# Solving the delta rule's triangular blocks of 16 instead of 8 by substitution, in a two-block transformer kernel

## The reference

```python
decay = jnp.exp(jnp.where(causal, g_cum[..., :, None] - g_cum[..., None, :], -jnp.inf))
k_beta = k * beta[..., None]
lower = jnp.where(strict, jnp.einsum('bhncd,bhnmd->bhncm', k_beta, k) * decay, 0.0)
t_inv = lax.linalg.triangular_solve(lower, eye, left_side=True, lower=True, unit_diagonal=True)
u = jnp.einsum('bhncm,bhnme->bhnce', t_inv, v * beta[..., None])
w = jnp.einsum('bhncm,bhnmd->bhncd', t_inv, k_beta * jnp.exp(g_cum)[..., None])
```

## Time and profile before

| | |
|---|---|
| median of three runs | 1306.01 us |
| the profiled execution's own time | 1305.88 us |
| its span, first to last instruction | 1304.5 us |
| PE busy | 1296.4 us, 99% |
| DVE busy | 931.3 us, 71% |
| ACT busy | 716.4 us, 55% |
| POOL busy | 89.8 us, 7% |
| TensorE's granted clock, mean | 0.999 of 2.4 GHz |
| the stage of the change, laps 0 to 7 | about 622 to 864 us |

### The profile page before, as it was taken

One profiled execution on the slowest core, in us unless ns is written; L12 is line 12 of the kernel. 1 busy time (PEld: TensorE's weight loads), 2 busy tenths in 40 slices (PEclk: granted clock), 3 DMA queues, 4 the chain that ended last, 5 costly groups with the idle time before them and its releaser, 6 DMA issues.

```text
span 1304.5 us, 23151 instructions
## 1 busy us (share of the span) xinstructions
PE 1296.4 (99%) x9404; PEld 1172.2 (90%) x9404; DVE 931.3 (71%) x1598; ACT 716.4 (55%) x1257; POOL 89.8 (7%) x181
## 2 busy tenths in 40 slices
PE   9999999999999999999999999999999999999998
PEld 8988999998879999989999999888999888989896
DVE  7866887777877977777877788864666555765553
ACT  7655665556666655547666666653343443644442
POOL 1000000000000000000122233300000000000000
PEclk9999999999999999999999999999999999999999
DMA  8443465543434655544444443556544444465540
GB/s 332 162 162 130 162 226 194 178 183 135 152 111 156 221 193 193 186 170 146 134 139 133 136 125 106 158 180 223 195 170 170 161 170 177 177 228 193 184 139 33
DMA packets 35036, 219.25 MB, mean 168 GB/s; under 512 B 4209, under 2 KB 7665, under 8 KB 9457
## 3 DMA queue, kind: packets, MB, share of 16 engines
q1 hardware_dynamic: 30608, 211.83, 44.7%
q10 hardware_dynamic: 4320, 5.94, 3.0%
HBM read 215.78 MB, written 1.05 MB: 166 GB/s over the span
## 4 chain that ended last, share of the span: by engine, by line
PE 96%; DVE 1%; ACT 1%; issue 0%; DMA 0%; SPq 0%; POOL 0%; ACTq 0%; DVEq 0%; POOLq 0%
PE bank L326 29%; PE bank L328 28%; PE bank L327 28%; PE bank L718 1%; PE bank L769 1%; PE bank L444 1%; PE bank L1756 1%; PE bank L1773 1%; PE bank L790 1%; DMA sb_x<-x 0%; PE bank L2445 0%; PE bank L712 0%; PE bank L1636 0%; PE bank L1912 0%; PE bank L1626 0%
## 5 line engine op out<-in xcount | busy, mean ns | idle before, releaser
L326 PE MATMUL bank<-sb_h_hi,sb_w_hi 128*128 128x256 f32 x1504 | 430.3, 286 | 0.0
L327 PE MATMUL bank<-sb_h_lo,sb_w_hi 128*128 128x256 f32 x1504 | 419.7, 279 | 0.0
L328 PE MATMUL bank<-sb_h_hi,sb_w_lo 128*128 128x256 f32 x1504 | 419.6, 279 | 0.0
L286 DVE TENSOR_TENSOR sb_w_lo<-sb_raw,sb_w_hi 128x1024 fp32r<-128x1024 f32 x185 | 226.2, 1223 | 105.7 <-ACT sb_w_hi L278 105.4
L326 PEld LDWEIGHTS bank<-sb_h_hi,sb_w_hi 128*128 128x128 f32 x1504 | 282.4, 188 | 5.5 <-issue 3.6
L327 PEld LDWEIGHTS bank<-sb_h_lo,sb_w_hi 128*128 128x128 f32 x1504 | 282.0, 188 | 2.8 <-issue 1.4
L328 PEld LDWEIGHTS bank<-sb_h_hi,sb_w_lo 128*128 128x128 f32 x1504 | 282.4, 188 | 0.0
L278 ACT CAST sb_w_hi<-sb_raw 128x1024 fp32r<-128x1024 f32 x188 | 197.0, 1048 | 100.0 <-PE bank L328 98.2
L289 DVE TENSOR_TENSOR sb_w_lo<-sb_raw,sb_w_hi 128x1024 fp32r<-128x1024 f32 x185 | 225.7, 1220 | 0.0
L279 ACT CAST sb_w_hi<-sb_raw 128x1024 fp32r<-128x1024 f32 x188 | 197.6, 1051 | 0.0
L326 PE MATMUL bank<-sb_w_hi,sb_h_hi 128*128 128x256 f32 (+1 forms) x512 | 161.2, 315 | 0.0
(11 more groups left out here) (378 smaller groups left out, 1922.2 us busy)
## 6 DMA issues: line engine op xcount, KB each, us to landing
sb_raw<-stream SPq DMA_DIRECT2D x199, 1024.0 KB, 4.8
sb_row<-rows ACTq DMA_DIRECT2D x3, 512.0 KB, 3.8
sb_x<-x SPq DMA_DIRECT2D x4, 256.0 KB, 4.5
sb_raw<-stream SPq DMA_DIRECT2D x2, 512.0 KB, 5.9
sb_norm_b<-norm_b ACTq DMA_DIRECT2D x4, 256.0 KB, 4.3
out<-sb_x SPq DMA_DIRECT2D x4, 256.0 KB, 2.0
sb_g_row<-sb_g_rows ACTq DMA_DIRECT2D x7, 128.0 KB, 6.3
sb_retain<-retain ACTq DMA_DIRECT2D x1, 768.0 KB, 4.2
```

The costliest lines, as they stand in the source:

```text
L286: V.tensor_tensor(w_lo[:, b, 0:HALF], raw[:, r, 0:HALF], w_hi[:, b, 0:HALF].bitcast(F32), ALU.subtract).then_inc(lo_done, 1)
L326: T.matmul(out_ap, l_hi, r_hi, start=start, stop=False, **kw)
L327: T.matmul(out_ap, l_hi, r_lo, start=False, stop=False, **kw)
L328: return T.matmul(out_ap, l_lo, r_hi, start=False, stop=stop, **kw)
```

## The change

Substitution goes on to blocks of 16: 30 steps in place of 14, rows of up to 15 elements in place of 7. One level of doubling goes (to 16 from 8), so two are left. The spread rows are 256 elements for each of the two chunks and no longer fit `z`. They are written to the second half of `row`, where the head's output `o` also stands, so DVE now waits for `o_turned` of the head two before. PE's spread product has 512 columns in place of 128. Masks are one fewer. The orders of all four engines are written anew around this: as a rule the first level comes four half steps later on PE.

```diff
-BASE = 8
-LEVELS = 5
-MASKS = 6
+BASE = 16
+LEVELS = 4
+MASKS = 5
...
-        spread = z[:].rearrange("p (t i j) -> p t i j", t=NT, i=BASE)
+        spread = row[:, 512:1024].rearrange("p (t i j) -> p t i j", t=NT, i=BASE)
...
+            need(V, o_turned, hd - 1)
             for t in range(NT):
                 ins = V.tensor_tensor(spread[:, t], diag[:, t:t + 1, :].to_broadcast([P, BASE, BASE]),
-                                      row8.unsqueeze(2).to_broadcast([P, BASE, BASE]), ALU.mult)
+                                      row16.unsqueeze(2).to_broadcast([P, BASE, BASE]), ALU.mult)
...
-            T.matmul(bank[7][:, 0:P], same8[:], z[:], start=True, stop=True).then_inc(spread_mm, 1)
+            T.matmul(bank[7][:, :], same16[:], row[:, 512:1024], start=True, stop=True).then_inc(spread_mm, 1)
...
-            rows = bank[7][:, 0:P].rearrange("p (t i j) -> p t i j", t=NT, i=BASE)
+            rows = bank[7][:, :].rearrange("p (t i j) -> p t i j", t=NT, i=BASE)
```

PE's order in laps 1 to 3 (`delta_pe`):

```diff
                 head_unit_pe(u, 0, 0, 1, tokens)
+                head_unit_pe(u, 0, 1, 3, tokens)
+                head_unit_pe(u, 0, 3, 5, tokens)
                 level_a_pe(hd, 1)
                 flip_v_pe(hd)
-                head_unit_pe(u, 0, 1, 3, tokens)
+                head_unit_pe(u, 0, 5, 7, tokens)
                 level_b_pe(hd, 1)
-                head_unit_pe(u, 0, 3, 5, tokens)
-                level_a_pe(hd, 2)
-                head_unit_pe(u, 0, 5, 7, tokens)
-                level_b_pe(hd, 2)
...
-                level_a_pe(hd, 3)
+                level_a_pe(hd, 2)
...
-                level_b_pe(hd, 3)
+                level_b_pe(hd, 2)
```

PE's in laps 4 to 6 (`delta_pe`):

```diff
             head_unit_pe(u, 1, 0, 4)
+            head_unit_pe(u, 1, 4, 6)
+            head_unit_pe(u, 1, 6, 8)
             level_a_pe(hd, 1)
             flip_v_pe(hd)
-            head_unit_pe(u, 1, 4, 6)
-            level_b_pe(hd, 1)
-            head_unit_pe(u, 1, 6, 8)
-            level_a_pe(hd, 2)
             u = unit_d(hd, 3)
             need(T, zs_done, hd)
             head_unit_pe(u, 2, 0, 1, tokens)
+            level_b_pe(hd, 1)
+            head_unit_pe(u, 2, 1, 3, tokens)
+            level_a_pe(hd, 2)
+            head_unit_pe(u, 2, 3, 5, tokens)
             level_b_pe(hd, 2)
-            head_unit_pe(u, 2, 1, 3, tokens)
-            level_a_pe(hd, 3)
-            head_unit_pe(u, 2, 3, 5, tokens)
-            level_b_pe(hd, 3)
```

DVE's in laps 4 to 6 (`delta_dve`):

```diff
             substitute_dve(hd)
             lo()
-            level_b_dve(hd, 1)
             older_dve(n, 0, 1)
             older_dve(n, 0, 2)
             older_dve(n, 0, 3)
-            level_b_dve(hd, 2)
+            level_b_dve(hd, 1)
             outputs_dve(hd - 1)
             query_sides_dve(hd)
             vbeta_dve(hd)
-            level_b_dve(hd, 3)
+            level_b_dve(hd, 2)
```

PE's in lap 7 (`gate_a_pe`):

```diff
+            T.wait_ge(zs_done, LAST)
+            square(u + 2, 0, KD, acts, (2, 1), 0)
+            square(u + 2, 0, KD, acts, (2, 1), 1)
             level_a_pe(hd, 1)
             flip_v_pe(hd)
-            T.wait_ge(zs_done, LAST)
-            square(u + 2, 0, KD, acts, (2, 1), 0)
-            level_b_pe(hd, 1)
-            square(u + 2, 0, KD, acts, (2, 1), 1)
-            level_a_pe(hd, 2)
             T.wait_ge(sig_a, 1)
             square(u + 2, 0, KD, acts, (2, 1), 2)
-            level_b_pe(hd, 2)
+            level_b_pe(hd, 1)
```

ACT's in lap 7 (`gate_a_act`):

```diff
             hi()
+            sig_act(0, (0, 1))
             level_a_act(hd, 1)
-            sig_act(0, (0, 1))
+            hi()
             level_a_act(hd, 2)
```

More of the change, by code:

```diff
@@ L73, in constants @@
     own[:, 0:BASE] = row % BASE == np.arange(BASE)[None, :]
-    own[:, BASE:2 * BASE] = row // BASE % (HB // BASE) == np.arange(HB // BASE)[None, :]
+    own[:, BASE:BASE + HB // BASE] = row // BASE % (HB // BASE) == np.arange(HB // BASE)[None, :]
     lev.append(own)
@@ L1386, in delta_begin_dve @@
             V.tensor_scalar(cap[:], upper[:], 1.0, -NEG, ALU.subtract, ALU.mult)
-            V.tensor_copy(same8[:], levels[:, MASKS - 2, :])
-            V.tensor_copy(own8[:], levels[:, MASKS - 1, 0:2 * BASE])
-            V.tensor_copy(x8[:], levels[:, MASKS - 1:MASKS, 0:BASE].to_broadcast([P, NT, BASE]))
+            V.tensor_copy(same16[:], levels[:, MASKS - 2, :])
+            V.tensor_copy(own16[:], levels[:, MASKS - 1, 0:2 * BASE])
+            V.tensor_copy(x16[:], levels[:, MASKS - 1:MASKS, 0:BASE].to_broadcast([P, NT, BASE]))
             V.memset(xtf[HALF_ROWS[1], :, 0:HB], 0.0).then_inc(begin_done, 1)
@@ L1720, in substitute_dve @@
                     if j:
[L1721 to L1725, removed]
+                        V.wait_ge(x16_step, steps * hd + NT * (j - 1) + t + 1)
+                    so_far = x16[:, t, j + 1:BASE] if j else row16[:, 1:BASE]
+                    V.scalar_tensor_tensor(x16[:, t, j + 1:BASE], rows[:, t, j + 1:BASE, j], x16[:, t, j:j + 1], so_far,
+                                           ALU.mult, ALU.add).then_inc(x16_step, 1)
+            V.wait_ge(x16_step, steps * (hd + 1))
             for t in range(NT):
-                ins = V.tensor_tensor(xt[:, t, :].rearrange("p (b i) -> p b i", i=BASE), x8[:, t:t + 1, :].to_broadcast([P, HB // BASE, BASE]),
-                                      block8.unsqueeze(2).to_broadcast([P, HB // BASE, BASE]), ALU.mult)
+                ins = V.tensor_tensor(xt[:, t, :].rearrange("p (b i) -> p b i", i=BASE), x16[:, t:t + 1, :].to_broadcast([P, HB // BASE, BASE]),
+                                      block16.unsqueeze(2).to_broadcast([P, HB // BASE, BASE]), ALU.mult)
             ins.then_inc(inv, 1)
@@ L1989, in first_lap_levels_pe @@
             head_unit_pe(u, 2, 0, 1, tokens)
+            level_a_pe(0, 1)
+            flip_v_pe(0)
+            head_unit_pe(u, 2, 1, 2, tokens)
+            level_b_pe(0, 1)
+            head_unit_pe(u, 2, 2, 4, tokens)
             level_a_pe(0, 2)
-            head_unit_pe(u, 2, 1, 2, tokens)
+            head_unit_pe(u, 2, 4, 5, tokens)
             level_b_pe(0, 2)
[L1993 to L1996, removed]
             head_unit_pe(u, 2, 5, 7, tokens)
@@ L2127, in delta_act @@
                 hi()
-                level_a_act(hd, 4)
+                level_a_act(hd, 3)
             else:
                 hi()
-                level_a_act(hd, 1)
                 outputs_act(hd - 1)
                 load_row_act(n)
+                hi_half(0)
+                level_a_act(hd, 1)
+                silu_act(n, 0)
                 level_a_act(hd, 2)
-                hi_half(0)
-                silu_act(n, 0)
+                newest_act(n, 1)
                 level_a_act(hd, 3)
-                newest_act(n, 1)
-                level_a_act(hd, 4)
                 store_act(hd - 1)
@@ L2220, in delta_pool @@
             blocks_pool(hd, 2)
-            if RAW_V + hd >= A_HEADS and hd < A_HEADS - 1:
-                blocks_pool(hd, 3)
-                outputs_pool(hd - 1)
-                return
             if hd:
                 outputs_pool(hd - 1)
-            blocks_pool(hd, 3)
         LAST = A_HEADS - 1
@@ L2295, in gate_a_act @@
             hi()
+            sig_act(0, (0, 1))
             level_a_act(hd, 1)
-            sig_act(0, (0, 1))
+            hi()
             level_a_act(hd, 2)
-            hi()
+            store_act(hd - 1)
             level_a_act(hd, 3)
-            store_act(hd - 1)
-            level_a_act(hd, 4)
             hi()
@@ L2320, in gate_a_dve @@
             lo_half(0)
+            lo_half(1)
             level_b_dve(hd, 1)
-            lo_half(1)
             vbeta_dve(hd)
+            store_dve(hd - 1)
             level_b_dve(hd, 2)
-            store_dve(hd - 1)
-            level_b_dve(hd, 3)
             lo()
```

22 lines of the change are left out of this document (8 added, 14 removed).

## The result

The changed kernel takes **1311.42 us** (median of 6 runs, 1309.71 to 1312.56) beside 1306.17 us (6 runs, 1305.94 to 1306.33) for the kernel before on the same chip: 5.25 us more, a ratio of 1.004 [1.003, 1.005]. The forecast was 1309.3, slower, in a range of 1304.0 to 1313.0. So the sign is right and the size is 2 us short.

What follows compares the result with a forecast made beforehand. PE was taken to bound the kernel (busy 99%, 96% of the chain). Terms +0.1 + 1.9 - 0.8 + 0.8 + 1.65 = +3.6 us, less 0.3 for overlap, +3.3 on the median 1306.01: 1309.3 us, range 1304.0 to 1313.0.

Steps and rivals of the forecast that it cites:

- PE's own work: All eight heads: one doubling level less gains 1.12 us, the wider spread product costs 0.61; net gain 0.51 a head.
- DVE's steps: DVE's substitution in each head: 0.134 us a step, so sixteen more steps add 2.15 us.
- Laps 1 to 3: Heads' stretches counted from 0: PE waits of 1.15 us against a gain of 0.51, each 0.64 slower, 1.9 in three.
- The second wait: In heads' stretches 1 to 3, PE waits 0.26 us for the second half of the next weights' low part.
- Laps 4 to 6: Heads' stretches 4 to 6: a 0.24 us wait at the second level product, each gains 0.27, 0.8 in three.
- ACT's late `nwt`: DVE ends later and ACT waits for it: 0.25 us charged at the start of stretches 5, 6 and 7, 0.8 together.
- Lap 0: First head's stretch: gains of 0.51 and 0.52 (`kdec` wait) against a new low-part wait of 1.09, sum +0.06 us.
- Lap 7: Last head's stretch, beside gate A: PE idles 2.15 us for ACT's table load and sigmoid; less 0.51, 1.65 slower.
- The drain of about 1.38 us: At the sigmoid's table switch: the skill's drain would make the wait 3.5 us, the kernel 1310.7; the forecast left it out.
- the 0.3 that was taken off for waits that overlap: Deduction of 0.3 us from the +3.6 sum, for waits at the start of a head's stretch and at its levels.
- PE's work alone: Rival: DVE and ACT always in time, kernel gains 4.1 + 0.5 us, 1301.4; chance 12%, with all below 1303.4.
- DVE as the bound: Rival: none of DVE's extra work hides in seven heads' stretches, +12 us, 1318; halfway 1313.5; chance 13%.

Runs made afterwards that it cites:

- the run with the steps in the old order: The kernel before with sixteen extra substitution steps of 7 elements a head on DVE, result unread; order, spread product and three levels stay: 1319.19 us, ratio 1.0100.
- the trace with fillers: Trace of the changed kernel with 18 extra unread PE products of 256 columns ahead of the sigmoid's wait in the last head's stretch: 1311.23 us, ratio 1.0036.

## Why the prediction was right in sign and short in size

- **PE's own work** (gain 1.12, loss 0.61 a head). The spread product's chain row is the 0.86 foreseen in laps 4 to 6, where PE goes on to weight products; in laps 1 to 3, where DVE waits for its end, it is 1.14 (forecast 1.02). The forecast's 4.9 us for it is PE's own time and not what the product costs the kernel: the run with the narrow product gives back 1.7 us, since in six of eight laps PE waits for DVE instead.
- **DVE's steps.** Thirty take 4.10 us on the chain, as forecast, 0.137 each against 0.134 for the narrower ones of before. The chain of lap 2:

```profile
693.58 1.14 PE bank L1712 x2
694.75 4.10 DVE sb_d_x L1724 x30
702.06 1.23 DVE sb_w_lo L306
```

- **Laps 1 to 3** (+0.64 each): +0.66, +0.66, +0.68. Aligned by PE's starts, lap 2 loses 0.98 us from ahead of the spread to behind it (forecast 0.41 + 0.61) and 0.60 at the low part (forecast 0.48). The second wait, forecast at 0.26, is 0.1 to 0.2. The low part on the chain above is the first half, forecast at 697.83 + 2.72 = 700.55; less the 1.47 us by which the lap itself starts later, it is at 700.59. One mechanism was missed: the spreading pair takes 1.07 us, not 1.00, as it runs beside POOL.
- **Laps 4 to 6** (-0.27 each, and 0.25 for ACT's late `nwt` from lap 5 on): -0.28, -0.12, -0.15. The second L1757 waits about 0.1, not 0.24. `nwt` is on PE's load queue three times, 0.2 us of it by PE's starts in lap 5:

```profile
PEld bank L1862 <- ACT sb_d_nwt L1857: 1.0, 3, 0.5
```

- **Lap 0** (+0.06): +0.22. `kdec`'s wait went and the low part's came, 1.17 instead of 1.09.
- **Lap 7** (+1.65). The failed step. The wait is 2.09 us (forecast 2.15), between a table load at 854.90 and the sigmoid at 856.19, 1.29 behind it. The drain of about 1.38 us that the Trainium skill, "ScalarE: Activation LUTs", section "What ACT_TABLE_LOAD costs", adds to a switch doesn't stand between them here either. I priced the wait at its own length. But a standstill of this length can bring the clock down to 1.2 GHz behind it: another 1.7 us in the profiled execution, 1.6 between the two sorts of executions. Since six of ten have it, the median should have about 1 us of it.
- **The remaining 0.5 us.** From 919 to 960 us, in the attention block's products of 256 columns, the traces of the changed kernel and of all variants but one take 0.5 us more than that of before with no wait anywhere, at full clock: from 931.70 to 942.81 in the one, from 937.70 to 949.25 in the other, 11.11 and 11.55 us for the same products. The run with 14 steps has the short time, like before, and the run with the steps in the old order has the long one, so it isn't the change's order that brings it. I know no cause, and whether it belongs to a kernel or to an execution is open.

The waits, +3.7 us (0.22 + 2.00 - 0.55 + 2.07 from the trace with fillers), came within half a microsecond of the forecast's +3.3. They are nearer to the +3.6 of its sum: no run shows the 0.3 that was taken off for waits that overlap. The low clock's 1 us and the 0.5 us above would make the rest; of these the first is shown and the second is open, so that the sum fits to 0.1 us is partly luck. Of the rivals, PE's work alone is refuted by the waits in the traces and by the run with the steps in the old kernel. DVE as the bound, at 1318, is what that run shows for the old order (1319.2), not for the change's.

## What to carry to other kernels

When an edit moves work past a point where PE waits for another engine, look first at what that engine needs from PE. Here four small products issued behind two blocks of work instead of ahead of them cost 3 us, more than half of the loss, and one moved line gave it back. Price a PE standstill of some 2 us with what its clock may do afterwards, and profile more than one execution before giving that price. And a cheaper product buys little where PE next waits for DVE. Ask of each saved microsecond at which wait it would be handed back.

## What was unexpected of the hardware

The clock behind a standstill. In the delta stage of this case's traces it fell to 0.50 behind waits of 1.71, 2.09, 2.09 and 2.77 us, each time for 3.41 or 3.42 us, beginning 0.35 to 1.6 us after PE had started again. It held behind two other waits of 2.09 us, and behind all of 1.36 us and less. Two windows of the run with the steps in the old kernel, PE idle and then at half clock with PE fully busy:

```profile
639.00:641.70 2.70, 0.00 (x0) 0.00 (x0) 2.63 (x17) 0.00 (x0) 0.00 (x0) 1.00 0.55 228
642.50:644.00 1.50, 1.50 (x9) 1.50 (x8) 1.50 (x2) 0.85 (x3) 0.78 (x1) 0.50 0.00 0
```

So the same code has executions with and without it, 1.6 us apart, which is a large part of why the changed kernel's first six runs spread over 2.9 us and those of the kernel before beside them over 0.4. It isn't all of it: each of the two sorts alone spreads over 1.3 to 1.4 us, and the larger groups of the kernel before over 1.0 to 1.6.

The second is what POOL does to DVE: an operation of 128x256 fp32 went from 0.42 to as much as 0.76 us beside a POOL operation on tiles of the same size. The Trainium skill, "GPSIMD Engine Reference", section "Specifications", says that POOL shares its SBUF interfaces with VectorE and that they contend where a DVE instruction has two SBUF inputs. L1703 has two, and the trace agrees.
